# Gated DeltaNet chunks in a decoder layer: lengths of q and k folded into masks, some transposes moved from TensorE to VectorE, and the second load of x moved to another queue

## The reference, cut to what matters

```python
q = l2_norm(q.reshape(B, T, GDN_HEADS, GDN_DK).astype(jnp.float32)) * (GDN_DK ** -0.5)
k = l2_norm(k.reshape(B, T, GDN_HEADS, GDN_DK).astype(jnp.float32))
...
decay = jnp.exp(jnp.where(tril, gc[..., :, None] - gc[..., None, :], -jnp.inf))
k_beta = k * beta[..., None]
v_beta = v * beta[..., None]
A = jnp.where(strict, jnp.einsum('bhncd,bhnsd->bhncs', k_beta, k) * decay, 0.0)
Tm = lax.linalg.triangular_solve(eye + A, jnp.broadcast_to(eye, A.shape), left_side=True, lower=True)
u = jnp.einsum('bhncs,bhnse->bhnce', Tm, v_beta)
w = jnp.einsum('bhncs,bhnsd->bhncd', Tm, k_beta * jnp.exp(gc)[..., None])
qk = jnp.where(tril, jnp.einsum('bhncd,bhnsd->bhncs', q, k) * decay, 0.0)
...
o = rms_norm(o, norm_w) * jax.nn.silu(zh)
```

## Time and profile before

| what | value |
|---|---|
| median of 3 runs | 1387.28 us (1387.07 to 1389.37) |
| the profiled execution's own time | 1385.52 us |
| its span, first to last instruction | 1383.8 us |
| TensorE busy | 1356.2 us (98%) |
| VectorE busy | 781.4 us (56%) |
| ScalarE busy | 625.5 us (45%) |
| GpSimd busy | 70.7 us (5%) |
| granted TensorE clock | 1.00 throughout |
| DMA | 240.48 MB, mean 174 GB/s |

### The profile page before, as it was taken

One profiled execution on the slowest core, in us unless ns is written; L12 is line 12 of the kernel. 1 busy time (PEld: TensorE's weight loads), 2 busy tenths in 40 slices (PEclk: granted clock), 3 DMA queues, 4 the chain that ended last, 5 costly groups with the idle time before them and its releaser, 6 DMA issues.

```text
span 1383.8 us, 18688 instructions
## 1 busy us (share of the span) xinstructions
PE 1356.2 (98%) x7067; PEld 1159.9 (84%) x7067; DVE 781.4 (56%) x909; ACT 625.5 (45%) x780; POOL 70.7 (5%) x94
## 2 busy tenths in 40 slices
PE   5999999999999999999999999999999999999998
PEld 5999988888887788888888888888888888888886
DVE  5568765576557465555555555444555555555554
ACT  5455543354344455544444444333444444444442
POOL 3001200033110000000000000000000000000000
PEclk9999999999999999999999999999999999999999
DMA  7555544444433465666666665566666666555564
GB/s 226 168 154 156 179 138 123 124 142 130 122 107 112 165 223 171 200 195 195 184 187 192 182 196 186 195 195 192 193 189 183 191 196 187 177 193 188 190 192 135
DMA packets 129415, 240.48 MB, mean 174 GB/s; under 512 B 12819, under 2 KB 13126, under 8 KB 129350
## 3 DMA queue, kind: packets, MB, share of 16 engines
q1 hardware_dynamic: 129248, 239.56, 57.4%
q10 hardware_dynamic: 102, 0.03, 0.0%
HBM read 237.45 MB, written 2.10 MB: 173 GB/s over the span
## 4 chain that ended last, share of the span: by engine, by line
PE 95%; DVE 2%; DMA 1%; ACT 1%; issue 0%; POOL 0%; SPq 0%; ACTq 0%; DVEq 0%
PE pair L485 25%; PE pair L483 25%; PE pair L484 25%; PE bg L627 4%; PE pair L651 3%; PE pair L652 3%; PE pair L653 3%; PE bg L611 1%; PE bg L706 1%; DVE w_lo L1029 1%; PE bg L519 1%; DMA h<-in_x_dram 1%; DMA raw<-in_w_o_dram 0%; ACT w_hi L769 0%; PE bg L608 0%; PE bg L613 0%
## 5 line engine op out<-in xcount | busy, mean ns | idle before, releaser
L1029 DVE TENSOR_TENSOR w_lo<-raw,w_hi 128x1024 fp32r<-128x1024 f32 x444 | 542.0, 1226 | 450.5 <-ACT w_hi L769 448.2
L769 ACT ACTIVATE w_hi<-raw 128x1024 fp32r<-128x1024 f32 x444 | 468.4, 1059 | 483.7 <-PE pair L485 438.1
L483 PE MATMUL pair<-w_hi,xT_hi 128*128 128x512 f32 x1088 | 435.2, 400 | 0.0
L485 PE MATMUL pair<-w_hi,xT_lo 128*128 128x512 f32 x1088 | 424.6, 390 | 0.0
L484 PE MATMUL pair<-w_lo,xT_hi 128*128 128x512 f32 x1088 | 423.7, 389 | 0.0
L485 PEld LDWEIGHTS pair<-w_hi,xT_lo 128*128 128x128 f32 x1088 | 204.2, 188 | 43.5
L484 PEld LDWEIGHTS pair<-w_lo,xT_hi 128*128 128x128 f32 x1088 | 204.8, 188 | 38.6
L483 PEld LDWEIGHTS pair<-w_hi,xT_hi 128*128 128x128 f32 x1088 | 204.6, 188 | 38.3
L483 PE MATMUL pair<-w_hi,actT_hi 128*128 128x512 f32 x352 | 137.7, 391 | 0.0
L485 PE MATMUL pair<-w_hi,actT_lo 128*128 128x512 f32 x352 | 137.1, 389 | 0.0
L484 PE MATMUL pair<-w_lo,actT_hi 128*128 128x512 f32 x352 | 137.0, 389 | 0.0
(11 more groups left out here) (215 smaller groups left out, 1068.1 us busy)
## 6 DMA issues: line engine op xcount, KB each, us to landing
raw<-in_w_in_dram SPq DMA_DIRECT2D x112, 512.0 KB, 3.8
raw<-in_w_gate_dram SPq DMA_DIRECT2D x88, 512.0 KB, 4.4
raw<-in_w_up_dram SPq DMA_DIRECT2D x88, 512.0 KB, 3.8
raw<-in_w_down_dram SPq DMA_DIRECT2D x88, 512.0 KB, 4.7
raw<-in_w_o_dram SPq DMA_DIRECT2D x32, 512.0 KB, 4.6
raw<-in_w_ple_gate_dram SPq DMA_DIRECT2D x32, 512.0 KB, 4.5
h<-in_x_dram SPq DMA_DIRECT2D x8, 512.0 KB, 6.6
raw<-in_w_ple_proj_dram SPq DMA_DIRECT2D x4, 512.0 KB, 5.8
```

Of the source, the lines that this page charges most:

```text
L483: mm(banks[t][:], hi[:, ts], wh, start=first, stop=False)
L485: m = mm(banks[t][:], lo[:, ts], wh, start=False, stop=last)
L769: f(w_hi[j % RING][:], raw[j % RING][:], ACT.Copy).then_inc(hi_ready, 1)
L1029: v.tensor_tensor(w_lo[j % RING][:], raw[j % RING][:], w_hi[j % RING][:].bitcast(F32), ALU.subtract).then_inc(lo_ready, 1)
```

## The change

It has four parts. First, q and k are no longer normalised. Their raw transposed forms in `ch` are multiplied directly (gramQ, gramA); the factor beta / |k|^2 goes into the triangular mask (`k_fac`, tile `TT`, on GpSimd), |k| scales v (`k_len`), and |q|^2 enters the output norm as its epsilon (`q_ms`), whose gain is multiplied by the root of 128 (`G_OG`). Steps q_n, k_n, qT, kT and kbT are gone. Second, after levels 0 to 4 T consists of blocks of at most 32, and VectorE's 32 x 32 block transpose (`flip`) makes the other tile; steps T0 and TT1 to TT4 are gone, TT5 stays on TensorE. The Y step now waits for the flip (`t_ready`). Third, the list of steps is shorter (114 in place of 148, of which some are empty rests), and it is spread over 140 slots in place of 144, the last four before U_WO being left out. Fourth, x is loaded again from ACT's queue, in four DMAs in a row at unit U_WO + 5; SP neither waits nor issues it.

```diff
-    steps = ["q_tok", "k_tok", "q_n", "v_tok", "k_n", "qT", "kT", "kbT", "gcrow", "gramQ", "gramA", "T0"]
+    steps = ["q_tok", "k_tok", "gcrow", "v_tok", "rest", "gramQ", "gramA"]
     for l in range(1, LEVELS - 1):
-        steps += [f"Y{l}", f"Z{l}", f"TT{l}"]
-    steps += [f"Y{LEVELS - 1}", "ZT"]
+        steps += [f"Y{l}", f"Z{l}"]
+    steps += [f"TT{LEVELS - 2}", f"Y{LEVELS - 1}", "ZT"]
     if b % 2:
-        steps += ["ks", "u", "qs", "o", "o_s", "rest", "o_n", "ogT"]
+        steps += ["ks", "u", "qs", "o", "rest", "o_s", "rest", "o_n", "rest", "ogT"]
     else:
-        steps += ["u", "S", "o", "o_s", "rest", "rest", "o_n", "ogT"]
+        steps += ["u", "S", "o", "o_s", "rest", "o_n", "ogT"]
...
-    slots += [(u, k) for u in range(U_Z + 4, U_WO) for k in range(2)]
+    slots += [(u, k) for u in range(U_Z + 4, U_WO - 2) for k in range(2)]
...
-                    if b == 1 and j % 2 == 0:
-
-                        if j == 0:
-                            for s in (("pv", HEADS - 2), ("pv", HEADS - 1), ("ogT", 2), ("ogT", 3)):
-                                wait_read(sp, s)
-                        n = j // 2
-                        sp.dma_start(h[:, :, n * CB:(n + 1) * CB], x_d[:, :, n * CB:(n + 1) * CB]).then_inc(x_again[n], 16)
...
                 if step == "q_tok":
                     pool.wait_ge(q_sum, b + 1)
-
-                    rstd(q_rs[c][:], q_ms[c][:], q_ss[c][:], float(P), P * EPS, q_rstd, b)
+                    g.tensor_tensor(B["Y"][:], over_heads(triu[:]), over_cols(sc["g"][:, c, hs]),
+                                    ALU.mult).then_inc(gtri_ready, 1)
                 elif step == "k_tok":
...
+                    pool.wait_ge(k_mean, b + 1)
+                    g.tensor_tensor(k_len[c][:], k_ms[c][:], root[:, 0:HG], ALU.pow).then_inc(len_ready, 1)
+                    pool.wait_ge(fac_ready, 2 * (b + 1))
+                    g.tensor_tensor(B["TT"][:], over_heads(triu[:]), over_cols(k_fac[c][:]),
+                                    ALU.mult).then_inc(ftri_ready, 1)
                 elif step == "gcrow":
                     pool.wait_ge(exp_ready, b + 1)
...
+                    pool.wait_ge(ftri_ready, b + 1)
+                    g.tensor_tensor(B["Y"][:], B["Y"][:], B["TT"][:], ALU.mult).then_inc(decay_ready, 1)
+                    if not c:
+                        wait_read(pool, ("k_tok", b))
+                        pool.wait_ge(decay_ready, b + 1)
+                        g.tensor_tensor(B["KD"][:], B["KD"][:], B["Y"][:, :, P - 1:P].to_broadcast([P, HG, P]),
+                                        ALU.mult).then_inc(kd_ready, 1)
...
-                elif step == "T0":
-                    pe.wait_ge(tt0, b + 1)
+                elif step[0] == "Y":
+                    pe.wait_ge(t_ready[c], (LEVELS - 2) * hg + min(int(step[1:]), LEVELS - 2))
+                    if step == f"Y{LEVELS - 1}":
+                        wait_read(pe, (f"TT{LEVELS - 2}", b))
...
-                            "gramQ": lambda: (B["AT"][:, j, :], ch[:, hd, ts]),
-                            "gramA": lambda: (B["AT"][:, j, :], ch[:, HEADS + hd, ts]),
+                            "gramQ": lambda: (ch[:, HEADS + hd, ts], ch[:, hd, ts]),
+                            "gramA": lambda: (ch[:, HEADS + hd, ts], ch[:, HEADS + hd, ts]),
...
+                if u == U_WO + 5:
+
+                    for s in (("pv", HEADS - 2), ("pv", HEADS - 1), ("ogT", 2), ("ogT", 3)):
+                        wait_read(act, s)
+                    for n in range(4):
+                        cs = slice(n * CB, (n + 1) * CB)
+                        act.dma_start(h[:, :, cs], x_d[:, :, cs]).then_inc(x_again[n], 16)
...
+            def flip(out, tile):
+
+                return v.transpose(out[:].rearrange("p h n -> p (h n)"), tile[:].rearrange("p h n -> p (h n)"))
...
                     v.reduce_sum(q_ss[c][:], B["T"][:], AX_X).then_inc(q_sum, 1)
-                elif step == "q_n":
-                    dve.wait_ge(q_rstd, 2 * (b + 1))
-                    read_out(s, v.tensor_tensor(B["Y"][:], bh, over_cols(q_rs[c][:]), ALU.mult))
+                    dve.wait_ge(q_sum, b + 1)
+                    v.tensor_scalar(q_ms[c][:], q_ss[c][:], float(P * P) * EPS, float(P * P) * EPS * EPS,
+                                    ALU.mult, ALU.add).then_inc(q_mean, 1)
...
                     v.reduce_sum(k_ss[c][:], B["TT"][:], AX_X).then_inc(k_sum, 1)
-                elif step == "k_n":
-                    dve.wait_ge(k_rstd, 2 * (b + 1))
-                    read_out(s, v.tensor_tensor(B["T"][:], bh, over_cols(k_rs[c][:]), ALU.mult))
+                    dve.wait_ge(k_sum, b + 1)
+                    v.tensor_scalar(k_ms[c][:], k_ss[c][:], EPS, None, ALU.add).then_inc(k_mean, 1)
+                    dve.wait_ge(k_mean, b + 1)
+                    v.reciprocal(k_inv[c][:], k_ms[c][:]).then_inc(fac_ready, 1)
+                    dve.wait_ge(fac_ready, 2 * b + 1)
+                    v.tensor_tensor(k_fac[c][:], k_inv[c][:], sc["beta"][:, c, hs], ALU.mult).then_inc(fac_ready, 1)
                 elif step == "v_tok":
                     wait_full(dve, s)
-                    read_out(s, v.tensor_tensor(B["V"][:], bh, over_cols(sc["beta"][:, c, hs]), ALU.mult))
+                    dve.wait_ge(len_ready, b + 1)
+                    read_out(s, v.tensor_tensor(B["V"][:], bh, over_cols(k_len[c][:]), ALU.mult))
...
                     v.tensor_tensor(B["TT"][:], over_heads(ident[:]), B["Y"][:], ALU.subtract).then_inc(tt0, 1)
+                    dve.wait_ge(tt0, b + 1)
+                    flip(B["T"], B["TT"]).then_inc(t_ready[c], 1)
...
                 elif step[0] == "Z":
+                    l = int(step[1:])
                     wait_full(dve, s)
                     read_out(s, v.tensor_tensor(B["T"][:], B["T"][:], bh, ALU.subtract))
+                    if l < LEVELS - 2:
+                        wait_read(dve, s)
+                        flip(B["TT"], B["T"]).then_inc(t_ready[c], 1)
...
                 elif step == "o_s":
                     dve.wait_ge(o_sq, b + 1)
                     v.reduce_sum(o_ss[c][:], B["Y"][:], AX_X).then_inc(o_sum, 1)
+                    dve.wait_ge(q_mean, b + 1)
+                    dve.wait_ge(o_sum, 2 * b + 1)
+                    v.tensor_tensor(o_ms[c][:], o_ss[c][:], q_ms[c][:], ALU.add).then_inc(o_sum, 1)
```

More of the change, by code:

```diff
@@ L391, in _ @@
             mask(g.memset(half[:], -0.5))
+            mask(g.memset(root[:], 0.5))
             mask(g.memset(ones[:], 1.0))
@@ L570, in delta @@
                     pass
[L571 to L576, removed]
                 elif step == "gcrow":
                     pe.wait_ge(gtri_ready, b + 1)
-                elif step == "gramQ":
-                    for s in ("qT", "kT", "kbT"):
-                        wait_read(pe, (s, b))
-                elif step == "gramA":
-                    pass
-                elif step == "T0":
-                    pe.wait_ge(tt0, b + 1)
+                elif step in ("gramQ", "gramA"):
+                    pass
+                elif step[0] == "Y":
+                    pe.wait_ge(t_ready[c], (LEVELS - 2) * hg + min(int(step[1:]), LEVELS - 2))
+                    if step == f"Y{LEVELS - 1}":
+                        wait_read(pe, (f"TT{LEVELS - 2}", b))
                 elif step == "ks":
@@ L608, in delta @@
                         last = tp(o, ch[:, base + hd, ts], ident[:])
-                    elif step in ("qT", "kT", "kbT", "T0", "ogT") or step.startswith("TT"):
-                        src = {"qT": "Y", "kT": "T", "kbT": "TT", "T0": "TT", "ogT": "V"}.get(step, "T")
-                        last = tp(o, B[src][:, j, :], ident[:])
+                    elif step == "ogT" or step.startswith("TT"):
+                        last = tp(o, B["V" if step == "ogT" else "T"][:, j, :], ident[:])
                     elif step == "gcrow":
-                        last = mm(o, ones[:], B["TT"][:, j, :], start=True, stop=True)
+                        last = mm(o, ones[:], B["Y"][:, j, :], start=True, stop=True)
                     else:
                         l, r = {
-                            "gramQ": lambda: (B["AT"][:, j, :], ch[:, hd, ts]),
-                            "gramA": lambda: (B["AT"][:, j, :], ch[:, HEADS + hd, ts]),
+                            "gramQ": lambda: (ch[:, HEADS + hd, ts], ch[:, hd, ts]),
+                            "gramA": lambda: (ch[:, HEADS + hd, ts], ch[:, HEADS + hd, ts]),
                             "Y": lambda: (B["AT"][:, j, :], B["T"][:, j, :]),
@@ L820, in post @@
                     wait_full(act, s)
-                    f(B["T"][:], bh, ACT.Square).then_inc(q_sq, 1)
+                    read_out(s, f(B["T"][:], bh, ACT.Square))
                 elif step == "k_tok":
                     wait_full(act, s)
-                    f(B["TT"][:], bh, ACT.Square).then_inc(k_sq, 1)
-                elif step == "qT":
-                    wait_full(act, s)
```

(16 more changed lines are left out.)

70 lines of the change are left out of this document (32 added, 38 removed).

## The result

The changed kernel takes 1368.32 us (median of 4 runs, 1367.73 to 1369.72) where the kernel before takes 1387.18 (4 runs, 1387.07 to 1389.37): 18.9 us less, ratio 0.9865, 95% interval 0.9853 to 0.9877. The forecast was 1367.6, its range 1364.5 to 1374.

The account below looks back on a forecast made before the run. TensorE, busy 98%, was taken to bound the kernel. 1385.5 - 14.8 (bursts) - 4.1 (ogT waits) - 1.8 (SP's wait) + 1.0 (new waits) = 1365.8 us; plus 1.76, 1367.6 us as a median, range 1364.5 to 1374.

Parts of the forecast that it names:

- Bursts: In TensorE's stream, 32 bursts of four transposes go, at 0.44 to 0.47 us each; gain 14.8 us.
- rival D: TensorE's freed place is filled by the split chain of ACT and VectorE; time within 0.2%, at 1386; chance 0.03.
- The load of x: At the first output projection weights, SP's wait goes, gain 1.8 us; x on ACT's queue delays no weights, cost 0.
- The wait at ogT of b = 3: TensorE's 2.90 us wait for VectorE's output norm goes, part of 4.1 us gained at ogT of b = 1 and 3.
- New waits at the flips: TensorE's Y steps wait for VectorE's transposes, tightest after gramA of b = 2; 1.0 us together, bounds 0 and 6.
- the 1.76 us between profile and median: Difference of the kernel before's median, 1387.28 us, from its profiled execution, 1385.52; added to the forecast's 1365.8 us.
- Rival C: VectorE's block transpose, time F, is slow between Z and Y; the gain is eaten from F = 4.5 us; chance 0.03.

Follow-up runs that it names:

- e5: The changed kernel with 24 more bursts of four TensorE transposes, one ahead of each Y burst and overwritten by it; 1378.36 us, ratio 0.9938.
- e1: The kernel before with only the second load of x moved to ACT's queue; 1384.92 us, ratio 0.9978.
- e4: The changed kernel with the second load of x back on SP between the w_o weights; 1371.83 us, ratio 0.9889.
- e8: The changed kernel with o_s and o_n of odd batches directly behind o and the three rests behind them; 1366.43 us, ratio 0.9848.
- e7: The changed kernel with each of VectorE's 20 transposes made four times; 1388.04 us, ratio 1.0003.
- e10: The kernel of e8 with one rest more behind gramA of b = 2; 1366.36 us, ratio 0.9853.
- e11: The kernel before with x on ACT's queue and o_n of the odd batches one slot earlier; 1383.49 us, ratio 0.9978.
- e2: The kernel before with only T0 and TT1 to TT4 moved to VectorE's block transposes, q and k still normalised; 1378.81 us, ratio 0.9934.
- e3: The changed kernel with T0 and TT1 to TT4 back on TensorE and ACT; 1380.13 us, ratio 0.9945.
- e6: The changed kernel with each of VectorE's 20 transposes made twice; 1369.84 us, ratio 0.9875.
- e9: The kernel of e8 with the second load of x back on SP; median 1368.70 us, ratio 0.9874.

## Why the prediction was right, step by step

**Bursts: right.** The forecast was 14.8 us for 32 bursts at 0.44 to 0.47. The stream of weight products became 14.5 us shorter without its waits, 0.45 us for a burst, and e5 has 0.443 for a burst next to another. Nothing filled the gap: rival D is out.

**The load of x: right in kind.** No weight is late while x lands (e1, e4). The Trainium skill ("DMA: Bandwidth & Descriptors", section "Issuing engines are not separate DMA queues") has DMAs of different engines on the same 16 engines. By that rule the queue itself gives nothing, and the trace agrees: with both queues loaded the engines moved 396 GB/s, where SP's queue alone moved 410 and 387 in two stretches of 2 us of e4, and what was gained is SP's wait. The prediction assumed that the two share evenly. From 460 to 463 us they nearly did, with 0.62 MB for x and 0.56 MB for the weights.

**The wait at ogT of b = 3: wrong.** "These take 7 x 1.36 = 9.5 us, and about 3 us more [...], 12.5 us, against the 11.8 us that the work needed under the same load." From o at 407.02 to the time ogT was due, 423.47 - 2.08 = 421.39, there were even 14.4 us, but the work took 16.4. The step that failed is to take the 11.8 us as a property of the work. In an order written out by hand a step begins when its turn comes. By `plan`, o_s stood one slot behind o and o_n three before the change; after it they stand two and five behind, because of the rest added ahead of o_s and the wider spread. Here 2.1 us of the forecast's 4.1 were not gained. e8 shows the cause: with o_s and o_n one and two slots behind o, and ogT where it was, that wait is gone, at the price of 0.6 us at pT.

**New waits at the flips: right.** 1.0 us was put on all such places. 0.36 us came, at Y1 of b = 2, the tight one that was named; 0.30 us more came at u of b = 3, which waits for no flip. VectorE got 15.5 us more rather than 12; 2.1 of it stands at the splits (544.1 against 542.0 us), for a reason that stays open.

**Median and profile: an addend that was misread.** I carried the 1.76 us between profile and median over to the changed kernel as if it were fixed. By size and by the granted clock it is a fall of the clock behind a wait of some 2 us or more, in a part of the executions. The profiled execution before had its waits of 2.90 and 1.83 us and no fall. The 46 executions of the kernel before that stand beside the experiments form four groups: 14 at 1385.4 to 1386.0 us with a mean clock of 0.999 on average, 18 at 1386.7 to 1387.5 with 0.998, 10 at 1388.1 to 1389.1 with 0.997 and 4 at 1389.9 to 1390.2 with 0.996. A fall that costs 1.7 us lowers the mean by 0.0012, so the steps fit one fall each, and the median has one. (This is an estimate from the sizes; none of the slower ones was profiled, and three falls are more than there are waits of 2 us.) After the change one such wait is left. One of four executions, 1369.72 with 0.998, looks like a fall; the two that make the median of 1368.32 have 0.999 and 1.000, so the 0.6 us between it and the profiled 1367.73 are something else, which stays open. With no such wait, in e8, the offset is nought. So two errors of the sum went against each other: 1.9 us too low for the profiled execution (1365.8 against 1367.73), 1.2 too high for the offset. The figure of 1367.6 is closer than its working deserved; that part is luck.

**The expectations of e1 and e4** were missed for the same reason: both took 1.8 us for the wait itself and nothing for the clock behind it, up to 1.7 us, and the runs gave 2.5 us in the one and 3.5 in the other.

**Rival C: right in kind, its turning point wrong.** It needs F = 4.5 us by the prediction's formula, and e7 has the gain used up at 2.85. The formula had no term for a split of VectorE (1.22 us) in between, as at 368.38 us in e7, ahead of the Z read whose Y then waited 1.34 us, nor for the clock. At the measured 0.71 none of this matters.

Two things stay open: what decides in a given execution whether the clock falls at a wait of 2 us, and why the 0.6 us at pT could not be dissolved; e10 is the only attempt at either.

## What to carry to other kernels

When one engine is busy 98% of the time, price a removed instruction by the distance between its neighbours in the timeline, and ask of each engine that takes it over only whether its slack at the tightest place holds. In an order written out by hand, put the slack behind the work, just ahead of the step that waits, not among the steps that produce: in e8 the same number of rests, moved, took a 2.1 us wait away and left 0.6 in another place. In e11, with only four slots from o to ogT, the same move gave 0.3 us at that step. And look at the spread of the executions: steps of 1.5 to 1.8 us between them pointed at waits whose cost is nearly twice what the list of waits says.

## What the runs showed that was not expected

A wait of TensorE of about 2 us can cost nearly its own length once more. In nine places of six profiled executions the granted clock was at about 0.5 (1.2 GHz) behind a wait of 2.90 (e1), 2.8 (e2), 3.5 (e3), 2.10 and 1.85 (e4), 2.6 us (e11), and three times in e7 (2.48, 2.60, 2.08); the products of 512 columns were then 0.43 us apart where they are 0.2267 at 2.4 GHz, for eight or so products, 1.7 us in all. In e1 the fall began 0.3 us before the wait was over, in e4 1.4 us behind it. Behind other waits of the same size, 2.90 and 1.83 us in the profiled execution before, 2.08 in the one after, in e5 and in e6, 2.1 in e2 and 1.92 in e9, it stayed at 1.00, as it did behind every wait of 1.5 us or less in these traces.

A block transpose of 128 x 512 float32 numbers on VectorE takes 0.711 to 0.713 us, hardly more than an elementwise instruction of that shape (0.682, the subtraction at Z). "VectorE: DVE Perf Modes" of the Trainium skill, section "The three transpose paths", gives 311 ns for 128 x 128 in bf16; four of those would be 1.24 us, an estimate from that page, and the measured 0.71 for four times the columns in one instruction decides here.
